# HGRN2 in a one-layer decoder trunk: the state steps of a head set between the levels of the next head, and the next head's forget gate and decay set in mid-head

## What is computed

```python
f = lb + (1.0 - lb) * jax.nn.sigmoid(f_raw)          # forget gate per channel; lb is 0 in this layer
logf, k = jnp.log(f), 1.0 - f
# for each chunk of tokens, S the state of the head (128 x 128):
G = jnp.cumsum(logf, axis=-2)
attn = einsum('bhtk,bhsk,bhtsk->bhts', q, k, exp(G_t - G_s))     # s <= t only
o = einsum('bhtk,bhkv->bhtv', q * exp(G), S) + einsum('bhts,bhsv->bhtv', attn, v)
S = S * exp(G_last) + einsum('bhsk,bhsv->bhkv', k * exp(G_last - G), v)
```

## Time and profile before

| | |
|---|---|
| time, median of 3 runs | 3148.82 us |
| the profiled execution: its time | 3150.24 us |
| its span | 3148.4 us |
| prompt part of HGRN2 | from about 1480 to 1663 us of the span |
| busy over the span: PE, PEld, DVE, ACT, POOL | 2599.2, 1999.1, 1190.4, 952.0, 497.6 us |
| mean granted clock of TensorE over the span | 0.901 of full speed |

### The profile page before, as it was taken

How to read it: one execution, slowest core, us unless ns; L and a number is a source line. 1 busy time by engine, 2 the same in 40 slices (tenths; PEclk the granted TensorE clock), 3 DMA queues, 4 the chain that set the end, 5 groups by cost and what they waited for, 6 DMA issues and landing times. The chain is left out here.

```text
span 3148.4 us, 39940 instructions
## 1 busy us (share of the span) xinstructions
PE 2599.2 (83%) x15210; PEld 1999.1 (63%) x15210; DVE 1190.4 (38%) x2286; ACT 952.0 (30%) x1575; POOL 497.6 (16%) x365
## 2 busy tenths in 40 slices
PE   6978788878975887598665799998989979999990
PEld 5965555558963786598553688887446436666660
DVE  1033166655526442201874111111332025565565
ACT  1022056652231322102441211111001135555555
POOL 2210000003320211432432111110001510000002
PEclk9989899998996798799896899999997989999995
DMA  5263130002101000210001211111120048898886
GB/s 210 81 168 93 33 119 25 1 30 81 47 9 57 1 2 5 101 45 21 1 1 64 106 48 40 40 50 46 64 110 41 1 167 332 340 356 340 337 327 241
DMA packets 88787, 328.90 MB, mean 104 GB/s; under 512 B 15921, under 2 KB 20556, under 8 KB 78852
## 3 DMA queue, kind: packets, MB, share of 16 engines
q1 hardware_dynamic: 71012, 265.80, 23.1%
q10 hardware_dynamic: 10256, 37.37, 3.0%
q0 software_dynamic: 7408, 24.23, 2.3%
HBM read 285.66 MB, written 45.89 MB: 105 GB/s over the span
## 5 line engine op out<-in xcount | busy, mean ns | idle before, releaser
L164 PE MATMUL ps<-mg_high,mg_wg 128*128 128x344 f32 x576 | 191.3, 332 | 41.2 <-POOL mg_wg L2051 41.2
L2631 DVE TENSOR_TENSOR ex_wg<-ex_rg,ex_wg 128x1024 fp32r<-128x1024 f32 x96 | 111.4, 1220 | 271.1 <-ACT ex_wg L2587 271.1
L166 PE MATMUL ps<-mg_low,mg_wg 128*128 128x344 f32 x576 | 184.7, 321 | 0.0
L165 PE MATMUL ps<-mg_high,mg_wg 128*128 128x344 f32 x576 | 184.6, 320 | 0.0
L2578 PE MATMUL ps<-ex_wd,ex_aT 128*128 128x512 f32 x368 | 163.4, 597 | 14.7 <-DVE ex_aT L2656 14.7
L2069 PE MATMUL ps<-o,mg_wb 128*128 128x344 f32 x576 | 170.4, 452 | 0.0
L164 PE MATMUL ps<-hx_high,hgp_w 128*128 128x344 f32 x384 | 123.7, 322 | 42.1 <-DVE hx_low L156 42.1
L164 PE MATMUL ps<-cv_high,dnp_w 128*128 128x344 f32 x384 | 124.2, 323 | 23.5 <-DVE cv_low L156 23.5
L2069 PEld LDWEIGHTS ps<-o,mg_wb 128*128 128x128 f32 x576 | 108.4, 190 | 52.4
L2183 PE MATMUL ps<-mo_w,mT 128*128 128x512 f32 (+1 forms) x288 | 128.0, 604 | 15.7 <-DMA mo_w<-in_w_out 15.7
L164 PEld LDWEIGHTS ps<-mg_high,mg_wg 128*128 128x128 f32 x576 | 109.2, 190 | 44.0 <-issue 41.8
(11 more groups left out here) (530 smaller groups left out, 6019.8 us busy)
## 6 DMA issues: line engine op xcount, KB each, us to landing
ex_rg<-in_w_eg SPq DMA_DIRECT2D x96, 512.0 KB, 8.7
ex_ru<-in_w_eu SPq DMA_DIRECT2D x96, 512.0 KB, 11.8
ex_wd<-in_w_ed SPq DMA_DIRECT2D x46, 1024.0 KB, 9.3
o<-in_cache SPq DMA_DIRECT2D x64, 256.0 KB, 4.3
mg_raw<-in_w_mg SPq DMA_DIRECT2D x24, 512.0 KB, 3.5
scratch_s_rows<-ex_ob ACTq DMA_DIRECT2D x23, 512.0 KB, 9.4
scratch_s_bias<-at_bv ACTq DMA_DIRECT2D x1, 8192.0 KB, 21.9
dnp_w<-in_w_dn SPq DMA_DIRECT2D x16, 512.0 KB, 3.5
```

The lines of the kernel that those rows point to most:

```text
L164: pe.matmul(out, w[:, 0, k, :], x.high[:, k, tokens], start=first, stop=False)
L165: pe.matmul(out, w[:, 1, k, :], x.high[:, k, tokens], start=False, stop=False)
L166: return pe.matmul(out, w[:, 0, k, :], x.low[:, k, tokens], start=False, stop=final)
L2631: dve.tensor_tensor(w[:, 1, piece(m)], raw[:, piece(m)], w[:, 0, piece(m)], ALU.subtract).then_inc(s[split], 1)
```

## The change

The loops of the four engines are written anew so that head h's levels and head h - 1's state steps go together:

- TensorE: step l of head h - 1 follows level l of head h (levels 0 to 6); step 7 follows the turning of the keys. The last head's steps stand at the end, as before.
- VectorE: the state of step l follows the mask of level l; step 7 follows the copy of `kt`. `decay` of the next head follows level 4.
- ScalarE: the output copies of head h - 1 follow the exponentials of levels 2 to 6, and three stand after level 6. `forget` of the next head (Abs, Exp, Ln) stands after the copy of `vt` in level 3, and the Sigmoid, now `complement`, after the exponential of level 5.
- GpSimd's program is unchanged; it starts on the next head when `decay` is done.
- `at`, `vt`, `qg`, `kt` and `eg` get a second buffer, by the head's parity.
- PSUM: levels, turned v and turned keys go through banks 0 to 3 as one ring of two pairs (`ring`, `place`, `claim`): each waits until the unit two places ahead of it has been read. The steps alone have banks 4 to 7.

ScalarE before, in head 1, from the copy of `vt` on: three exponentials of levels 4 to 6, `forget` with the Sigmoid, the eight output copies, then the next head (hg_vt is `vt`, hg_E the level's `E`, hg_lf the gate on its way to log f, hg_z here the gate that becomes k, o the output).

The diff, cut; TensorE's old program stands above:

```diff
@@ -1810,16 +1810,21 @@
...
-            at = s2("at", [P, NBLK, P])
-            vt = s2("vt", [P, NBLK, P])
-            qg = s2("qg", [P, TP])
+            at = s2("at", [P, 2, NBLK, P])
+            vt = s2("vt", [P, 2, NBLK, P])
+            qg = s2("qg", [P, 2, TP])
...
-            kt = s2("kt", [P, NBLK, P])
-            eg = s2("eg", [P, NBLK])
+            kt = s2("kt", [P, 2, NBLK, P])
+            eg = s2("eg", [P, 2, NBLK])
...
+            ring = [u for h in range(H4) for u in
+                    [("L", h, -1), ("L", h, 0), ("L", h, 1), ("V", h, 0)] + [("L", h, l) for l in range(2, LEV)] + [("K", h, 0)]]
+            place = {u: k for k, u in enumerate(ring)}
+            pair = lambda *u: ps[:, 2 * (place[u] % 2):2 * (place[u] % 2) + 2, :]
+            chunk = lambda i: slice(i * BLK, (i + 1) * BLK)
...
@@ -1842,10 +1847,21 @@
...
+                def complement(h):
+                    k = z[:, 4 + h]
...
+                def output(h, i):
+                    n = h * NBLK + i
+                    act.wait_ge(s["ou"], n + 1)
+                    act.activation(o[:, h, chunk(i)], ps[:, 6 + n % 2, 0:P], ACT.Copy).then_inc(s["oc"], 1)
...
+                complement(0)
                 for h in range(H4):
                     for l in range(LEV):
...
@@ -1853,19 +1869,24 @@
...
                         if l == 1:
...
-                            act.activation(qg[:], Gs[:, h % 2, 0:TP], ACT.Exp).then_inc(s["fs"], 1)
+                            act.activation(qg[:, h % 2], Gs[:, h % 2, 0:TP], ACT.Exp).then_inc(s["fs"], 1)
                         if l == 2:
...
                         if l == 3:
...
-                            act.activation(bank2(vt[:]), ps[:, 4:6, :], ACT.Copy).then_inc(s["vtc"], 1)
-                    if h + 1 < H4:
-                        forget(h + 1)
-                    for i in range(NBLK):
-                        n = h * NBLK + i
-                        act.wait_ge(s["ou"], n + 1)
-                        act.activation(o[:, h, i * BLK:(i + 1) * BLK], ps[:, 6 + n % 2, 0:P], ACT.Copy).then_inc(s["oc"], 1)
+                            act.activation(bank2(vt[:, h % 2]), pair("V", h, 0), ACT.Copy).then_inc(s["vtc"], 1)
+                            if h + 1 < H4:
+                                forget(h + 1)
+                        if l == 5 and h + 1 < H4:
+                            complement(h + 1)
+                        if h and l >= 2:
+                            output(h - 1, l - 2)
+                    if h:
+                        for i in range(LEV - 2, NBLK):
+                            output(h - 1, i)
+                for i in range(NBLK):
+                    output(H4 - 1, i)
...
             def _(pool):
@@ -1919,15 +1940,21 @@
...
-                    src = ps[:, 2 * (m % 2):2 * (m % 2) + 2, :]
+                    src = pair("L", h, l)
                     mask = (c.ident[:] if l < 0 else up[:, l, :].bitcast(I32)).unsqueeze(1).unsqueeze(1).to_broadcast([P, 2, 4, P])
...
-                    dst = at[:].rearrange("p (a b) t -> p a b t", a=2)
+                    dst = at[:, h % 2].rearrange("p (a b) t -> p a b t", a=2)
                     if l < 0:
...
+                def state(h, i):
+                    n = h * NBLK + i
+                    dve.wait_ge(s["ou"], n + 1)
+                    dve.scalar_tensor_tensor(S[:, h, :], S[:, h, :], eg[:, h % 2, i:i + 1], ps[:, 4 + n % 2, 0:P], ALU.mult, ALU.add).then_inc(s["Su"], 1)
...
@@ -1948,65 +1975,90 @@
...
+                        if h:
+                            state(h - 1, l)
+                        if l == 4 and h + 1 < H4:
+                            decay(h + 1)
...
-                    link(dve.tensor_copy(eg[:], qg[:, BLK - 1:TP:BLK]))
-                    dve.tensor_tensor(qg[:], qg[:], q, ALU.mult).then_inc(s["qg"], 1)
+                    link(dve.tensor_copy(eg[:, h % 2], qg[:, h % 2, BLK - 1:TP:BLK]))
+                    dve.tensor_tensor(qg[:, h % 2], qg[:, h % 2], q, ALU.mult).then_inc(s["qg"], 1)
...
-                    dve.tensor_copy(bank2(kt[:]), ps[:, 6:8, :]).then_inc(s["ktc"], 1)
-                    if h + 1 < H4:
-                        decay(h + 1)
-                    for i in range(NBLK):
-                        n = h * NBLK + i
-                        dve.wait_ge(s["ou"], n + 1)
-                        dve.scalar_tensor_tensor(S[:, h, :], S[:, h, :], eg[:, i:i + 1], ps[:, 4 + n % 2, 0:P], ALU.mult, ALU.add).then_inc(s["Su"], 1)
+                    dve.tensor_copy(bank2(kt[:, h % 2]), pair("K", h, 0)).then_inc(s["ktc"], 1)
+                    if h:
+                        state(h - 1, NBLK - 1)
+                for i in range(NBLK):
+                    state(H4 - 1, i)
...
             def _(pe):
+                def claim(*u):
+                    k = place[u]
+                    if k >= 2:
+                        m, j, l = ring[k - 2]
+                        if m == "L":
+                            pe.wait_ge(s["mk"], j * NL + l + 2)
+                        else:
+                            pe.wait_ge(s["vtc" if m == "V" else "ktc"], j + 1)
+                    out = pair(*u)
+                    return lambda i: out[:, i // 4, (i % 4) * P:(i % 4 + 1) * P]
+                def level(h, l):
+                    n = h * LEV + l
+                    if l >= 0:
+                        pe.wait_ge(s["Z"], n + 1)
+                    out = claim("L", h, l)
+                    for i in range(NBLK):
+                        t = chunk(i)
+                        x, y = (Z[:, n % 2, t], Z[:, n % 2, t]) if l >= 0 else (z[:, 4 + h, t], z[:, h, t])
+                        mm = pe.matmul(out(i), x, y, start=True, stop=True)
+                    mm.then_inc(s["mm"], 1)
+                def values(h):
+                    out = claim("V", h, 0)
+                    for i in range(NBLK):
+                        t_ = pe.transpose(out(i), z[:, 8 + h, chunk(i)], c.ident[:])
+                    t_.then_inc(s["vt"], 1)
+                def keys(h):
+                    pe.wait_ge(s["kd"], h + 1)
+                    out = claim("K", h, 0)
+                    for i in range(NBLK):
+                        t_ = pe.transpose(out(i), kd[:, chunk(i)], c.ident[:])
+                    t_.then_inc(s["turned"], 1)
+                def step(h, i):
+                    n = h * NBLK + i
+                    if i == 0:
+                        pe.wait_ge(s["mk"], (h + 1) * NL)
+                        pe.wait_ge(s["vtc"], h + 1)
+                        pe.wait_ge(s["ktc"], h + 1)
+                        pe.wait_ge(s["qg"], h + 1)
+                    if n >= 2:
+                        pe.wait_ge(s["oc"], n - 1)
+                        pe.wait_ge(s["Su"], n - 1)
+                    pe.matmul(ps[:, 4 + n % 2, 0:P], kt[:, h % 2, i, :], vt[:, h % 2, i, :], start=True, stop=True)
+                    if n:
+                        pe.wait_ge(s["Su"], n)
+                    pe.matmul(ps[:, 6 + n % 2, 0:P], S[:, h, :], qg[:, h % 2, chunk(i)], start=True, stop=False)
+                    pe.matmul(ps[:, 6 + n % 2, 0:P], vt[:, h % 2, i, :], at[:, h % 2, i, :], start=False, stop=True).then_inc(s["ou"], 1)
...
                 for h in range(H4):
...
+                    level(h, -1)
+                    for l in range(LEV):
+                        level(h, l)
+                        if h:
+                            step(h - 1, l)
                         if l == 1:
...
+                            values(h)
+                    keys(h)
                     if h:
...
+                        step(h - 1, NBLK - 1)
+                for i in range(NBLK):
+                    step(H4 - 1, i)
         recurrent_samples(c, "hgs", dr["state_hg"], dr["o_hg_s"], o, z[:, 0:4, TP:T], z[:, 4:8, TP:T], z[:, 8:12, TP:T],
                           lambda h, b, n: f[:, h, b:b + n])
```

More of the change, by code:

```diff
@@ L1968, in _ @@
                     pe.wait_ge(s["k"], h + 1)
-                    for l in range(-1, LEV):
-                        m, n = h * NL + l + 1, h * LEV + l
-                        if l >= 0:
-                            pe.wait_ge(s["Z"], n + 1)
-                        if m >= 2:
-                            pe.wait_ge(s["mk"], m - 1)
-                        for i in range(NBLK):
-                            t = slice(i * BLK, (i + 1) * BLK)
-                            x, y = (Z[:, n % 2, t], Z[:, n % 2, t]) if l >= 0 else (z[:, 4 + h, t], z[:, h, t])
-                            mm = pe.matmul(ps[:, 2 * (m % 2) + i // 4, (i % 4) * P:(i % 4 + 1) * P], x, y, start=True, stop=True)
-                        mm.then_inc(s["mm"], 1)
-                        if l == 1:
-                            if h:
-                                pe.wait_ge(s["Su"], NBLK * h)
-                            for i in range(NBLK):
-                                t_ = pe.transpose(ps[:, 4 + i // 4, (i % 4) * P:(i % 4 + 1) * P], z[:, 8 + h, i * BLK:(i + 1) * BLK], c.ident[:])
-                            t_.then_inc(s["vt"], 1)
```

(24 more changed lines are left out.)

## The result

| | before | after |
|---|---|---|
| time, median of 5 runs | 3148.43 us | 3132.86 us (3121.49 to 3136.03) |
| ratio, 95% interval | | 0.9944 (0.9925 to 0.9964) |
| the profiled execution: time, span | 3150.24, 3148.4 us | 3128.20, 3126.4 us |
| HGRN2 prompt stage, first scan to last state step | 175.2 us | 162.2 us |

What follows compares the result with a forecast made beforehand. VectorE was taken to set the pace inside a head's levels and to starve between heads. Terms -36.7 + 8.3 + 9.6 + 0.4 + 6.0 + 3.9 = -8.5 us gave 3140.4 us, range 3136.0 to 3147.0.

Steps and rivals of the forecast that it cites:

- chains gone, 24 steps in the row: Three chains of eight state steps stop standing alone, -29.6 us; 24 steps in VectorE's row cost 0.345 each, +8.3.
- factors' waits for ScalarE (restart, level 4, level 6): VectorE's restart between heads goes, -7.1 us; waits at level 4 add 9.6 and ahead of level 6 0.4.
- TensorE's clock: Seam levels after TensorE's pauses run at a lower clock: 1.3 us for each of three seams, +3.9, bounds 0 and 9.
- GpSimd term: GpSimd's moved work holds VectorE at level 6, the `kd` product and the next head's first factors: +6.0 us, bounds 2 and 9.6.
- ScalarE at level 4: VectorE waits for level 4's exponential, behind the next head's `forget`: 2.8 us in head 0, 3.4 in heads 1 and 2.
- The Sigmoid at level 5: Sigmoid through level 6's exponential, 3.7 us, is almost covered by VectorE's `decay`, 3.6; 0.1 a head, 0.4 in all.
- a wait at the masks: Sign of being wrong: VectorE waiting for TensorE at the masks would point to the clock, (a) or (b).
- Rival (a): TensorE's clock stays low from level 6 through the next head's level 1: 9 us instead of 3.9, 3145.4 us; chance 0.24.
- (b): TensorE becomes the bound, its lower clock holding all through heads 1 to 3: 3157 us; chance 0.05.
- (c): The wait at level 4 does not arise because ScalarE gets ahead: 9.6 us more gained, 3131; chance 0.05.
- (d): Each of 24 steps waits 1 us on VectorE for its `ou`: about 3148 us if half; chance 0.05.
- (e): Table switches cost ScalarE twice the load's row: 3.8 us a seam, 11.5 in all, 3151.9 us; chance 0.01.

Runs made afterwards that it cites:

- split: Changed kernel with the Ln of the next head's gate moved from level 3 to level 5, ahead of its Sigmoid; 3122.16 us, ratio 0.9925, stage 152.0 us.
- pool_late: Changed kernel with GpSimd's first subtraction for the next head made to wait for the factors of level 6; 3126.42 us, ratio 0.9933, stage 159.2 us.
- split_kd2: As split, with a second buffer for `kd`; 3120.30 us, ratio 0.9913, stage 148.7 us.
- all_three: The edits of split, split_kd2 and pool_late together; 3118.40 us, ratio 0.9923, stage 148.8 us.
- split_warm: As split, with level 5 of heads 0 to 2 multiplied twice by TensorE in its pause; 3118.40 us, ratio 0.9914, stage 151.2 us.

## Why the prediction was wrong

The direction, the mechanism and its places were right; the sum was 4.5 us short in the stage, and the remaining 2.6 us are outside it. The terms, against what the stage showed. Measured values are sums over VectorE's rows, an instruction counted from its start to its end or to the next start, idle time apart:

| term | predicted | measured |
|---|---|---|
| chains gone, 24 steps in the row | -29.6 + 8.3 = -21.3 | idle 29.3 to 7.3, steps 11.0 to 9.4: -23.6 |
| factors' waits for ScalarE (restart, level 4, level 6) | -7.1 + 9.6 + 0.4 = +2.9 | 11.3 to 14.7: +3.4 |
| GpSimd's work beside the factors and `kd` | +6.0 | 52.2 to 53.1 and 4.6 to 5.8: +2.1 |
| TensorE's clock (masks) | +3.9 | 0.1 to 5.3: +5.1 |
| sum | -8.5 | -13.0 |

**The step that failed is the GpSimd term**, +6.0 us in the sum and +2.1 in the stage, mis-sized by 3.9 us. At level 6 I had both factors held by D(0), 2.0 us a seam. VectorE and GpSimd in order of time:

```profile
1509.22 0.66 DVE L1936 TENSOR_TENSOR hg_Z<-hg_z,hg_E 128x512 f32<-128x512 f32 x1
1509.80 1.52 DVE L1937 TENSOR_TENSOR hg_Z<-hg_z,hg_E 128x512 f32<-128x512 f32 x1
```

```profile
1509.38 1.40 POOL L1904 TENSOR_TENSOR hg_E<-hg_Gs 128x512 f32<-128x512 f32 x1 [6.83 <-DVE hg_Gs L1926]
1510.74 1.48 POOL L1905 TENSOR_TENSOR hg_E<-hg_Gs 128x512 f32<-128x512 f32 x1
```

VectorE goes from the scan straight to the first factor, at 1509.22; GpSimd, let go by the same scan, starts at 1509.38, and its first instruction takes 1.40 us instead of 1.04: it is the one that is held. VectorE is held once, in the second factor (1.52 instead of 0.69). GpSimd's second instruction then meets the mask, which takes its usual 1.30. That is 0.8 us a seam, not 2.0, and 3.5 of the 3.9; most of the rest is the lead that the steps give GpSimd, worth some 4.4 us and not 3.6. I had asked who runs at that time, and not who comes first. No run lets GpSimd go first at level 6, so that reading rests on the order of these rows. The other two places were sized right: the `kd` product +0.4, the first factors +1.7. The term's lower bound, 2, had been set for one factor held at each place, and there the sum came out.

At the first factors it made no difference who came first. In head 1 VectorE did (1518.86 against 1519.02), and its second factor was held; in head 2 GpSimd did, and the first factor was held:

```profile
1558.89 1.89 POOL L1911 TENSOR_TENSOR hg_kd<-hg_Gs 128x1024 f32<-128x1024 f32 x1 [4.25 <-DVE hg_kt L1987]
```

The pair took 2.90 and 2.87 us. GpSimd has one instruction there and two at level 6.

**The steps** were charged 0.345 us each, their duration, but start to start a step in the row takes 0.28 (0.26 in the row above where the next factor starts at 1558.99 after 1558.73): 1.6 us of the 2.3. The rest is the last head's own chain, which the sum left as it was: it waited 1.2 us less for TensorE, against 0.5 us that small gaps at the 24 steps took back.

**ScalarE at level 4**: 3.08, 3.98 and 4.00 us of idle time where 2.8, 3.4 and 3.4 were forecast. The split run shows that it was the Ln with its two loads, and that nothing took its place. **The Sigmoid at level 5**: covered, as worked out; 1548.60 against 1548.63.

**TensorE's clock**: TensorE at level 6 of head 0, at levels 0 and 1 of head 1, and at level 1 of head 3:

```profile
1511.38 3.61 PE L2015 MATMUL ps<-hg_Z 128*128 128x128 f32 x16 [5.10 <-DVE hg_Z L1937]
...
1521.89 3.64 PE L2015 MATMUL ps<-hg_Z 128*128 128x128 f32 x16 [3.38 <-DVE hg_Z L1937]
...
1526.04 1.95 PE L2015 MATMUL ps<-hg_Z 128*128 128x128 f32 x16
...
1606.23 2.40 PE L2015 MATMUL ps<-hg_Z 128*128 128x128 f32 x16
```

After pauses of 5.10 and 3.38 us a level takes 3.61 and 3.64 us, at a granted clock of 0.53 and 0.54, the lower level for nearly all of it. The size taken, 1.3 a seam, was 0.4 too small. The prediction had named a wait at the masks as a sign of being wrong, though its own sum held 3.9 us of it. Rival (a), that the clock stays low through level 1, did not come in heads 1 and 2, where level 1 takes 1.95 and 1.99 us. In head 3 it came in part: level 1 takes 2.40 (the last row, granted clock 0.80), and the masks of levels 0 to 2 wait 1.7 us, a third of all their waits. In (b) TensorE never became the bound, (c) was not seen, and in (d) no step waited.

**The table switch (e)**: Ln ends at 1535.12, the copy runs in between, the load takes 1535.29 to 1536.57, and the exponential starts at 1536.59. The drain that the Trainium skill, "ScalarE: Activation LUTs", section "What ACT_TABLE_LOAD costs", adds to a load does not show here either, and the gain at split, 10.2 us, is accounted for without it (idle time ahead of the factors 14.7 to 3.8).

**The range** was set by this stage alone. With the stage's true sum on the median the forecast would have stood at 3135.8, just below the range; with the GpSimd term alone put right, at 3136.4, just inside it. The median came 3.0 us below 3135.8 (2.6 if the kernel before is taken at its five-run median). That is within the interval of the ratio, and the unedited repeat measured 13.0 us, no more than the stage's own, so it is not shown to come from the change: it may be scatter alone. The first three runs of before, within 0.5 us of one another, had made me take the rest of the kernel for fixed. Two slips in the prediction's arithmetic carry no weight: 3140.3 stands rounded as 3140.4, and half of rival (d) would give 3152, not 3148.

## What to carry to other kernels

When work that stood alone moves beside other work, look for the engine that has to make the next input in time: here the gain came from the steps alone, and the largest cost came from one Ln with two table loads that stood ahead of an exponential which VectorE needed. Where two engines exclude each other, ask for each pair of instructions which of the two is let go first, and how often each can then be held: VectorE, coming first, was held once and not twice at level 6. Moving such a collision (pool_late) gained next to nothing by itself, since it came back beside other instructions. A function that needs its own table is best placed next to others that end in a switch anyway: the same Ln ahead of the Sigmoid cost one load less and no wait.

## What the runs showed of the hardware

- Three runs within 0.5 us don't bound a kernel of this length: later runs of the same kernel spread over 17 us. The shorter ones are those with the higher granted clock of TensorE over the run: of the kernel before, in the comparisons of the experiments, the seven runs at 0.900 took 3146.9 to 3154.2 us, and the four at 0.906 and 0.907 took 3136.9 to 3138.3. What sets the clock of a run was not tested. Between the two profiles of the changed kernel the stages ahead of the changed one differ by 9.7 us and that one by 0.01.
- A copy of 8 columns on VectorE (`eg`) takes 0.17 us alone. Where it meets a subtraction of GpSimd that started ahead of it, it ended with that one: 0.52 us in split_kd2, 0.66 in pool_late, and 1.68 and 1.84 in all_three, where GpSimd ends at 1552.63 and the copy at 1552.66.
- The length of TensorE's pause alone doesn't tell the clock of the level behind it. In the changed kernel levels took 3.64 and 3.61 us after pauses of 3.38 and 5.10 us, and 3.61 after one of 2.76 (level 4 of head 1); in split a level took 2.05 after a pause of 2.98 (level 0 of head 1). In split_warm 1.8 us more of work ahead of a pause of 3.5 us brought the next level to 2.54 and 3.19 us in two heads, and in a third it stayed at 3.78 after a pause of 3.80.
